# The last attention rounds beside the output projection, narrow products in halves, and an opening with its weight remainders on VectorE

## The chip, the cores and the metric

The kernel runs on one core of one Trainium2 chip. The metric is the device time of one execution in microseconds (us), as the median of three runs. One further execution was recorded by the hardware profiler; all rows below come from it.

## The reference

One inference step of a trunk of four layers, for a prompt of 256 positions and eight samples of one position each (264 columns together), width 1024. Each layer is a mixer and a SwiGLU feed-forward, each with a norm before and after and a residual sum. The mixers are retention (layers 0 and 3), pooling (layer 1) and dilated attention (layer 2):

```
for i in range(DEPTH):                       # 4
    kind, j = i % 3, i // 3
    hp, hs = rms_norm(xp, g[0]), rms_norm(xs, g[0])
    ...                                      # mixer(kind) of hp and of hs
    xp = xp + rms_norm(mp, g[1])
    xp = xp + rms_norm(swiglu(rms_norm(xp, g[2]), w_ffn_in[i], w_ffn_out[i]), g[3])
    ...                                      # the same for xs

# attention: 3 dilation groups (128, 1), (512, 4), (2048, 16), 16 heads of 64
proj = (xn @ w_in).reshape(B, L, G, 3, ATT_HEADS, ATT_DH)
    ...                                      # per group: scores + ALiBi bias, masked softmax, values
wts = jnp.stack(ls) * jnp.exp(m_all - jnp.max(m_all, axis=0))
o = jnp.einsum('gblh,gblhe->blhe', wts, jnp.stack(outs)) / jnp.sum(wts, axis=0)[..., None]
return o.reshape(B, L, D_MODEL) @ w_out, new_kv
```

For the prompt the keys are the prompt's own; for each of the eight samples they are rows of three caches and the sample's own row. Everything is float32.

## The kernel before

**Weights.** The activations stand with features on partitions and the 264 columns along the free axis. The weights come in units, mostly of 1024 x 256 (1 MB). SyncE loads unit u into one of three `raw` buffers as soon as the remainder of unit u - 3 is done (L404). To keep float32's accuracy, a unit is split in two: ScalarE rounds it to `w_hi` (`hi(u)`, L428), and VectorE or GpSimd computes the remainder `w_lo` = raw - w_hi (`lo(u)`, L917 and L1383). Which of them does it is set by the list `on_pool`: mostly odd units on GpSimd, in the retention layers nearly all. `w_hi` and `w_lo` have three buffers each; `hi(u)` waits until unit u - 3 has been used. The activations are split likewise (`g_hi`, `g_lo`).

**Projections.** A unit gives 256 output features, two halves t of 128, each in a bank of a pair of PSUM banks `acc`. `proj` issues, for each t and each of the eight input features blocks k, w_hi x g_hi and w_hi x g_lo (L1476, L1477), and then the w_lo x g_hi products (L1483): 48 products of 264 columns. Behind each t of the first pass, and behind t = 0 of the second, a function of a list `between` may issue other work. VectorE reads the banks.

**Queues.** Each engine has one stream, written out by hand; the engines meet in semaphores. There is no planner: the order in each stream is the order of the source. So an instruction waits behind everything before it on its engine.

**Opening.** TensorE first runs eight products of identity and ones (L1562) while the input lands, transposes the input (L1571, L1572), and then runs the high products of units 0 and 1 (`proj_first`, L1583, L1584). The column sums of the squares follow (`pre_stat`, L1538), then the low products of both units (L1590). VectorE copies the transposes (L1008, L1009), makes `g_lo` (L929), the remainder of unit 0, and two sums of squares (`pre_sum` L938, `pre_rest` L944) for which the column sums wait; unit 1's remainder is GpSimd's.

**Attention.** Sub-layer 4 has 36 input units, nine for each quad of four heads: query, key and value of three groups. They are steps n of 0 to 35. Each quad has eight rounds i (a head and a half of the prompt). A round is a chain over three engines: scores (PE, L1875), bias (DVE, L1248) and maximum (L1251), exp (ACT, L777), inverse of the sum (DVE, L1256), scaling (ACT, L783), three or six transposes (PE, L1859), their copy `pT` (ACT, L789), value products (PE, L1847), their copy `y` (DVE, L1239). `round_at(n)` says which round starts at step n; the eight rounds of a quad are spread over the steps of the next quad's units, with scores at n, transposes at n + 1, values at n + 2. From the second transpose on bank 1 they wait for the values of the round before to be copied.

The samples' attention of a quad, `decode(q, s)`, runs in steps s = 0 to 8 of the next quad, called on TensorE through `between`. Steps 1 to 4 spread two queries each over the partitions, and VectorE multiplies and sums them with the cached keys (L1269, L1272); steps 5 and 6 are the softmax; steps 7 and 8 are the value products, 16 each of 128x4 outputs with the cached values as stationary operand (L1914, two records each), in one block behind the first t of the projection.

For the last quad there is no next quad. Its first round starts at step 35; rounds 25 to 31 run in a loop of their own, `for i in range(24, 32)`, in which round i's transposes, round i - 1's values and round i + 1's scores stand beside one `decode(3, s)`. Scores alternate between the two pairs of `acc` banks. Behind the loop come the four units of the output projection: unit 0 in pieces (features 0 to 3, then the last round's values, then 4, 5, then 6, 7), as the attention's output features are split by `ao_hi` (ACT, L821) and `ao_lo` (DVE, L1305), and units 1, 2 and 3 whole (the last by `proj_last`). ScalarE does `hi(uo + p + 2)` ahead of unit p's square and gains (`post_square`), VectorE `lo(uo + p + 2)` ahead of reading unit p's banks (`post_evac`).

## Time and profile before

| | us |
|---|---|
| median of 3 runs | 1932.83 (1932.66 to 1934.03) |
| the profiled execution | 1937.19 |
| its span | 1935.4 |
| TensorE busy in the span | 1849.3 |
| VectorE, ScalarE, GpSimd busy | 1042.3, 911.4, 778.8 |
| mean granted TensorE clock | 0.966 |

The span is the time from the first to the last instruction; the profiled execution's own time has a little around it. Busy time of TensorE says nothing of its rate: the clock is granted at one of two levels, 1.2 or 2.4 GHz, and the windows below carry it as PEclk, with 1.00 for the full rate and 0.50 for the half. A record is one instruction as the profiler saw it; a float32 matmul shows as two records, a transpose as one.

### The profile page before, as it was taken

How to read it: one execution, taken by the hardware profiler on the slowest of the kernel's cores; microseconds unless marked ns; L12 is line 12 of the kernel's file. 1: busy time of each engine (PE TensorE's matmuls, PEld its weight loads, DVE VectorE, ACT ScalarE, POOL GpSimd, SP SyncE). 2: the span in 40 equal slices, each digit the busy share in tenths (PEclk: the TensorE clock that was granted, in tenths of full speed). 3: DMA queues.
4: the chain of work that ended last, by engine and by line, in shares of the span. 5: the costliest groups of instructions: out<-in, count | busy, mean ns of one | idle time of the engine just before them, and what ended most of it. 6: DMA issues, size and time to landing. Idle time of an engine off the chain costs nothing.

```text
span 1935.4 us, 32448 instructions
## 1 busy us (share of the span) xinstructions
PE 1849.3 (96%) x14116; PEld 1781.6 (92%) x14116; DVE 1042.3 (54%) x1119; ACT 911.4 (47%) x1064; POOL 778.8 (40%) x226
## 2 busy tenths in 40 slices
PE   8999989999979999999999979999999999899997
PEld 7999989999879999989989969999999999899997
DVE  5455554764487745354545452776354545647753
ACT  5556555343553344353434433544455555553333
POOL 5455435554224443412211200345455545355541
PEclk9999989999989999999999977999999999899999
DMA  8766855555335555844545521355667678545552
GB/s 266 251 227 245 290 176 172 175 174 180 104 109 177 182 184 167 244 149 134 162 135 154 143 69 43 127 184 164 189 229 238 231 252 294 184 143 175 174 180 83
DMA packets 306036, 346.33 MB, mean 179 GB/s; under 512 B 7847, under 2 KB 269479, under 8 KB 305887
## 3 DMA queue, kind: packets, MB, share of 16 engines
q1 hardware_dynamic: 257968, 260.36, 42.9%
q10 hardware_dynamic: 47927, 83.90, 12.6%
q8 instruction: 112, 1.84, 0.4%
q14 instruction: 29, 0.24, 0.0%
HBM read 299.66 MB, written 44.82 MB: 178 GB/s over the span
## 4 chain that ended last, share of the span: by engine, by line
PE 81%; DVE 9%; ACT 4%; issue 3%; DMA 2%; ACTq 1%; PEldq 0%; DVEq 0%
PE acc L1476 20%; PE acc L1477 20%; PE acc L1483 20%; PE mix L1914 2%; PE mix L1616 2%; PE mix L1875 1%; PE mix L1538 1%; DMA out_dram<-st 1%; PE acc L1504 1%; PE mix L1847 1%; ACT w_hi L428 1%; PE acc L1505 1%; PE acc L1510 1%; PE mix L1628 1%; DVE st L1029 1%
## 5 line engine op out<-in xcount | busy, mean ns | idle before, releaser
L1383 POOL TENSOR_TENSOR w_lo<-raw,w_hi 128x2048 fp32r<-128x2048 f32 (+2 forms) x163 | 695.1, 4268 | 728.6 <-ACT w_hi L428 728.6
L1476 PE MATMUL acc<-g_hi,w_hi 128*128 128x264 f32 x2576 | 658.0, 293 | 9.5 <-DVE gate L1172 3.2
L1477 PE MATMUL acc<-g_lo,w_hi 128*128 128x264 f32 x2576 | 646.8, 288 | 0.0
L428 ACT ACTIVATE w_hi<-raw 128x2048 fp32r<-128x2048 f32 (+3 forms) x260 | 455.9, 1755 | 166.7 <-PE acc L1483 78.3
L917 DVE TENSOR_TENSOR w_lo<-raw,w_hi 128x2048 fp32r<-128x2048 f32 (+1 forms) x97 | 376.2, 3878 | 270.4 <-ACT w_hi L428 270.4
L1476 PEld LDWEIGHTS acc<-g_hi,w_hi 128*128 128x128 f32 x2576 | 493.5, 192 | 18.5 <-issue 13.0
L1477 PEld LDWEIGHTS acc<-g_lo,w_hi 128*128 128x128 f32 x2576 | 496.4, 193 | 1.2
L1483 PE MATMUL acc<-g_hi,w_lo 128*128 128x264 f32 x2576 | 351.1, 287 | 0.0
L1483 PEld LDWEIGHTS acc<-g_hi,w_lo 128*128 128x128 f32 x2576 | 333.9, 190 | 1.5
L1416 POOL TENSOR_TENSOR h_lo<-hid,h_hi 128x528 fp32r<-128x528 f32 x44 | 59.2, 1344 | 333.5 <-ACT h_hi L702 333.5
L1476 PE MATMUL acc<-h_hi,w_hi 128*128 128x264 f32 x664 | 164.1, 284 | 0.0
L1477 PE MATMUL acc<-h_lo,w_hi 128*128 128x264 f32 x664 | 164.0, 285 | 0.0
L699 ACT ACTIVATE silu_gate<-gate 128x528 f32<-128x528 f32 x44 | 28.4, 646 | 281.9 <-DVE gate L1172 281.9
L1477 PEld LDWEIGHTS acc<-h_lo,w_hi 128*128 128x128 f32 x664 | 125.1, 188 | 0.0
L1476 PEld LDWEIGHTS acc<-h_hi,w_hi 128*128 128x128 f32 x664 | 125.0, 188 | 0.0
L1029 DVE SCALAR_TENSOR_TENSOR st<-mix,k_s,st 128x512 f32<-128x512 f32 x128 | 89.9, 744 | 6.2 <-ACT st L526 3.3
L1483 PE MATMUL acc<-h_hi,w_lo 128*128 128x264 f32 x664 | 90.7, 285 | 0.0
L1038 DVE SCALAR_TENSOR_TENSOR tq<-st,rq,mix 128x512 f32<-128x512 f32 x64 | 47.8, 747 | 71.3 <-ACT mix L537 45.1
L1483 PEld LDWEIGHTS acc<-h_hi,w_lo 128*128 128x128 f32 x664 | 84.9, 189 | 0.0
L526 ACT ACTIVATE st<-st 128x1024 f32<-128x1024 f32 x64 | 67.1, 1052 | 20.7 <-DMA st<-in_state_ret_dram 11.7
L1616 PEld LDWEIGHTS mix<-tbase,tq 128*128 128x128 f32 x512 | 65.4, 199 | 6.7 <-DVE tq L1038 4.0
L1616 PE MATMUL mix<-tbase,tq 128*128 128x1 f32 x512 | 64.4, 247 | 4.8 <-DVE tq L1038 4.7
(232 smaller groups left out, 2427.2 us busy)
## 6 DMA issues: line engine op xcount, KB each, us to landing
raw<-in_w_ffn_in_dram SPq DMA_DIRECT2D x88, 1024.0 KB, 5.3
raw<-in_w_in_ret_dram SPq DMA_DIRECT2D x48, 1024.0 KB, 6.8
raw<-in_w_in_attn_dram SPq DMA_DIRECT2D x36, 1024.0 KB, 5.5
st<-in_state_ret_dram ACTq DMA_DIRECT2D x64, 512.0 KB, 6.6
out_dram<-st ACTq DMA_DIRECT2D x64, 512.0 KB, 6.0
raw<-in_w_ffn_out_dram SPq DMA_DIRECT2D x32, 768.0 KB, 4.9
raw<-in_w_ffn_out_dram SPq DMA_DIRECT2D x32, 640.0 KB, 5.1
raw<-in_w_out_ret_dram SPq DMA_DIRECT2D x16, 1024.0 KB, 6.9
```

What stands on the lines that cost most here:

```text
L428: A(w_hi[:, u % SPL, 0:size[u]], raw[:, u % RAW, 0:size[u]], ACT.Copy).then_inc(hi_split, 1)
L526: A(st[:, g % ST], st[:, g % ST], ACT.Copy, scale=GAMMA[n // 8]).then_inc(st_scaled, 1)
L917: TT(w_lo[:, u % SPL, 0:size[u]], raw[:, u % RAW, 0:size[u]], w_hi[:, u % SPL, 0:size[u]].bitcast(F32), ALU.subtract).then_inc(lo_by_dve, 1)
L1029: ins = STT(st[:, g % ST, kt, :], mix[:, 2, :], k_s[:, n // 8 % 2, kt, b:b + 1], st[:, g % ST, kt, :], ALU.mult, ALU.add)
L1038: STT(tq[:], st[:, g % ST, 1, :], rq[:, n // 8 % 2, 1, SEQ + b:SEQ + b + 1], mix[:, 3, :], ALU.mult, ALU.add).then_inc(t_ready, 1)
L1383: TT(w_lo[:, u % SPL, 0:size[u]], raw[:, u % RAW, 0:size[u]], w_hi[:, u % SPL, 0:size[u]].bitcast(F32), ALU.subtract).then_inc(lo_by_pool, 1)
L1416: TT(h_lo[:, 2 * j:2 * j + 2, :], hid[:, j % 2], h_hi[:, 2 * j:2 * j + 2, :].bitcast(F32), ALU.subtract).then_inc(h_lo_ready, 1)
L1476: MM(out, wh, x_hi[:, ks[k], :], start=first and k == 0, stop=False)
L1477: MM(out, wh, x_lo[:, ks[k], :], start=False, stop=False)
L1483: ins = MM(acc[:, 2 * (pair % 2) + t, 0:T], w_lo[:, u % SPL, o:o + P], x_hi[:, ks[k], :], start=False, stop=last and k == len(ks) - 1)
L1616: ins = MM(mix[:, 0, vt * 8 + b:vt * 8 + b + 1], tq[:, vt * P:(vt + 1) * P], ones[:, 0:1], start=True, stop=True)
L1914: ins = MM(out, vc[:, b, x, t * P:(t + 1) * P], dPT[:, x, 4 * b:4 * b + 4], start=(x == 0), stop=(x == 1))
```

## The change

Four things change.

1. **Opening.** Unit 1's remainder is VectorE's (`on_pool`), issued behind the sum for the column sums. The products ahead of the input go from eight to four.
2. **Narrow products.** `decode` of steps 7 and 8 takes `parts`: four samples behind t = 0 of the unit's high products and four behind t = 1.
3. **Last quad.** The rounds of the last quad follow the spread of the others: steps 36 to 44 take the place of the loop, with scores at n, values of n - 2 and transposes of n - 1. Scores 25 to 31 go to the one pair of `acc` banks that output unit 1 uses later, and wait for the bias of the round before. Output unit 0 is started in the other pair: features 0 to 3 at steps 38 to 41, and features 4 and 5 at steps 43 and 44, between the halves of the narrow products. Behind the steps come unit 1's features 0 to 5, unit 0's 6 and 7, unit 1's 6 and 7, then units 2 and 3. VectorE puts the inverse between its two sample products, and copies the values behind the second. ScalarE issues `row_out(23)` behind the first scaling, and the new value rows' DMAs behind the next exp.
4. **`hi(uo + 2)`** moves from behind the last features' split to step 43.

```diff
-        on_pool += [n == 0 if next_pooled and n < 2 else
+        on_pool += [n == 0 if next_pooled and n < 2 else sub > 0 and u % 2 == 1 if n < 2 and not after else
...
-            return 8 * (m // 9) + m % 9 if m >= 0 and m % 9 < 8 else None
+            return 8 * (m // 9) + m % 9 if 0 <= m < 36 and m % 9 < 8 else None
+        def out_k_at(n):
+            return {38: 0, 39: 1, 40: 2, 41: 3, 43: 4, 44: 5}.get(n)
...
-            wide_bank = mix[:, 2:4, :] if i <= 24 else acc[:, 2 * (i % 2):2 * (i % 2) + 2, :]
+            late = (pair_at[ATT_SUB, "out"] + 1) % 2
+            wide_bank = mix[:, 2:4, :] if i <= 24 else acc[:, 2 * late:2 * late + 2, :]
...
# ScalarE
+                scaled(24)
                 row_out(23)
-                new_rows(3, 1)
-                decode(3, 0)
-                for i in range(24, 32):
...
+                for n in range(36, 45):
+                    if round_at(n) is not None:
+                        exps(round_at(n))
+                    decode(3, n - 36)
+                    if n == 36:
+                        new_rows(3, 1)
...
+                    if round_at(n) is not None:
+                        scaled(round_at(n))
+                    if 36 <= n < 42:
+                        ao_hi(n - 36)
+                    if round_at(n - 1) is not None:
+                        turned_out(round_at(n - 1))
+                    if n == 43:
+                        hi(uo + 2)
...
# VectorE
+                if sub == 0:
+                    lo(1)
                 lo(where[sub, "in"] + 2)
...
+                for n in range(36, 45):
+                    if round_at(n) is not None:
+                        biased(round_at(n))
+                    decode(3, n - 36, (0,))
+                    if round_at(n) is not None:
+                        inverse(round_at(n))
+                    decode(3, n - 36, (1,))
+                    if round_at(n - 2) is not None:
+                        pv_evac(round_at(n - 2))
+                    decode_end(3, n - 36)
+                    if 36 <= n < 42:
+                        ao_lo(n - 36)
...
# TensorE
-            for j in range(8):
+            for j in range(4):
                 MM(mix[:, 3, 0:P], ident, ones, start=True, stop=True)
...
-                        if i >= 27:
-                            pe.wait_ge(sc_biased, i - 1)
+                        pe.wait_ge(sc_biased, i)
...
-                        for b in range(DECB):
+                        for b in [4 * part + j for part in parts for j in range(4)]:
...
+                        split = (lambda: decode(quad - 1, s, (0,)), lambda: decode(quad - 1, s, (1,)))
                         proj(u0 + n, p0 + n, g_hi, g_lo, KK,
-                             between=(lambda: decode(quad - 1, s),) if quad else ())
+                             between=split if quad and s >= 7 else (lambda: decode(quad - 1, s),) if quad else ())
...
+                def out_part(p, ks, last=False):
+                    u, pair = uo + p, po + p
+                    pe.wait_ge(hi_split, u + 1)
+                    pe.wait_ge(lo_by_pool if on_pool[u] else lo_by_dve, lo_count[u])
+                    pe.wait_ge(acc_read, pair - 1)
+                    for k in ks:
+                        ao_wait(k)
+                        for t in range(2):
+                            out, at = acc[:, 2 * (pair % 2) + t, 0:T], k * UC + t * P
+                            wh = w_hi[:, u % SPL, at:at + P]
+                            MM(out, wh, g_hi[:, k, :], start=(k == 0), stop=False)
+                            MM(out, wh, g_lo[:, k, :], start=False, stop=False)
+                        for t in range(2):
+                            at = k * UC + t * P
+                            ins = MM(acc[:, 2 * (pair % 2) + t, 0:T], w_lo[:, u % SPL, at:at + P], g_hi[:, k, :],
+                                     start=False, stop=(k == KD - 1))
+                    if last:
+                        ins.then_inc(unit_done, 1)
...
+                for n in range(36, 45):
+                    if round_at(n) is not None:
+                        scores(round_at(n))
+                    if n > 36:
+                        decode_read(3, n - 37)
+                    decode(3, n - 36, (0,) if n >= 43 else (0, 1))
+                    if out_k_at(n) is not None:
+                        out_part(0, [out_k_at(n)])
+                    if n >= 43:
+                        decode(3, n - 36, (1,))
+                    if round_at(n - 2) is not None:
+                        values(round_at(n - 2))
+                    if round_at(n - 1) is not None:
+                        turn_probs(round_at(n - 1))
+                decode_read(3, 8)
                 pe.wait_ge(sc_biased, 32)
...
+                out_part(1, range(6))
+                out_part(0, (6, 7), last=True)
+                out_part(1, (6, 7), last=True)
+                proj(uo + 2, po + 2, g_hi, g_lo, KK)
                 proj_last(uo + 3, po + 3, g_hi, g_lo, KK, first=True)
```

## Rows read from the trace of the kernel before

**Rows 1.** The page, engines: busy us (share of the span) x instructions.

```profile
PE 1849.3 (96%) x14116; PEld 1781.6 (92%) x14116; DVE 1042.3 (54%) x1119; ACT 911.4 (47%) x1064; POOL 778.8 (40%) x226
```

**Rows 2.** TensorE's waits, whole span: waiting line, releaser: total us, times, longest.

```profile
PE mix L1859 <- DVE y L1239: 9.3, 9, 2.5
...
PE mix L1538 <- DVE sq L944: 2.7, 1, 2.7
```

**Rows 3.** Windows, opening: stretch, length, busy by engine (instructions), PEclk, DMA, GB/s.

```profile
13.00:21.00 8.00, 7.70 (x61) 7.45 (x62) 7.93 (x14) 7.99 (x12) 3.88 (x1) 1.00 0.49 147
...
24.40:32.10 7.70, 7.68 (x43) 7.28 (x44) 2.63 (x3) 2.46 (x3) 4.37 (x2) 0.78 0.93 300
```

**Rows 4.** Timeline, opening, several engines: start, us, instruction, [idle before <-releaser].

```profile
16.48 2.29 DVE L917 TENSOR_TENSOR w_lo<-raw,w_hi 128x2048 fp32r<-128x2048 f32 x1
...
17.12 6.68 POOL L1383 TENSOR_TENSOR w_lo<-raw,w_hi 128x2048 fp32r<-128x2048 f32 x1 [16.68 <-ACT w_hi L428]
...
18.68 0.71 DVE L938 TENSOR_TENSOR sq<-sq 128x528 f32<-128x528 f32 x1
...
19.09 1.90 ACT L428 ACTIVATE w_hi<-raw 128x2048 fp32r<-128x2048 f32 x1
...
19.43 4.94 DVE L944 TENSOR_TENSOR sq<-sq 128x528 f32<-128x528 f32 x1
...
24.42 1.76 PEld L1538 LDWEIGHTS mix<-sq,tbase 128*128 128x128 f32 x8 [2.95 <-DVE sq L944]
...
26.36 5.59 PE L1590 MATMUL acc<-g_hi,w_lo 128*128 128x264 f32 x32
```

**Rows 5.** Tile tbase, up to 15 us: ns min/median/max of warm-up, then transposes.

```profile
L1562 PE MATMUL mix<-tbase x16: 420/421/582, 4.9 to 8.3; 128*128 128x128 f32 x16
...
L1571 PE MATMUL mix<-tbase,y x16: 272/300/341, 8.7 to 12.7; 128*128 128x128 f32 x16
```

**Rows 6.** Windows around the narrow blocks of quads 1 to 3.

```profile
899.00:913.00 14.00, 13.87 (x93) 13.63 (x92) 5.35 (x9) 3.65 (x4) 0.00 (x0) 0.76 0.42 139
998.00:1010.00 12.00, 11.87 (x89) 11.63 (x88) 2.24 (x7) 4.13 (x5) 4.57 (x1) 0.86 0.22 74
1012.00:1022.00 10.00, 10.00 (x75) 9.96 (x75) 3.33 (x4) 0.99 (x3) 0.00 (x0) 0.83 0.57 149
1098.00:1108.00 10.00, 9.87 (x71) 9.63 (x71) 3.80 (x7) 2.92 (x4) 0.00 (x0) 0.83 0.31 109
1108.00:1120.00 12.00, 12.00 (x92) 11.96 (x91) 1.03 (x3) 2.93 (x3) 4.54 (x1) 0.86 0.43 118
```

**Rows 7.** Timeline of TensorE: a narrow block, a retention query; and a window around that.

```profile
1109.85 3.63 PE L1914 MATMUL mix<-sq,vc 128*128 128x4 f32 x32
...
132.04 1.02 PE L1616 MATMUL mix<-tbase,tq 128*128 128x1 f32 x8 [0.41 <-DVE tq L1038]
...
100.00:150.00 50.00, 48.86 (x370) 45.58 (x369) 23.69 (x31) 29.12 (x32) 24.10 (x7) 1.00 0.68 233
```

**Rows 8.** The last quad: three windows, and TensorE's longest waits from 1121 to 1184.

```profile
1121.00:1168.00 47.00, 36.15 (x160) 28.71 (x161) 29.29 (x58) 19.96 (x45) 0.00 (x0) 0.69 0.14 38
1168.00:1190.00 22.00, 22.00 (x105) 22.00 (x105) 1.38 (x6) 2.11 (x3) 0.00 (x0) 0.50 0.00 1
...
PE mix L1847 <- ACT pT L789: 4.2, 2, 3.3
PE mix L1859 <- DVE y L1239: 3.7, 3, 1.9
```

**Rows 9.** Timeline, output projection, three engines.

```profile
1198.03 2.13 PE L1483 MATMUL acc<-g_hi,w_lo 128*128 128x264 f32 x16
...
1198.73 1.90 ACT L428 ACTIVATE w_hi<-raw 128x2048 fp32r<-128x2048 f32 x1
...
1200.70 4.62 POOL L1383 TENSOR_TENSOR w_lo<-raw,w_hi 128x2048 fp32r<-128x2048 f32 x1 [85.39 <-ACT w_hi L428]
...
1203.88 2.13 PE L1483 MATMUL acc<-g_hi,w_lo 128*128 128x264 f32 x16
```

More of the change, by code:

```diff
@@ L854, in att_mixer @@
                         act.wait_ge(dpv_read, 6)
-                    if i < 30:
-                        ao_hi(i - 24)
-                    decode(3, i - 23)
+                    if round_at(n) is not None:
[6 more added lines that the diff above has]
+                        hi(uo + 2)
                 act.wait_ge(kv_stored, 16 * 12)
@@ L863, in att_mixer @@
                 for p in range(4):
-                    hi(uo + p + 2)
+                    if p:
+                        hi(uo + p + 2)
                     post_square(sub, p)
@@ L1256, in inverse, with decode @@
                     nc.vector.reciprocal(rl[:, i % 2:i % 2 + 1], lsum[:, i % 2:i % 2 + 1]).then_inc(rl_ready, 1)
-                def decode(q, s):
-                    if s == 0:
+                def decode(q, s, parts=(0, 1)):
+                    if s == 0 and 0 in parts:
                         dve.wait_ge(qs_hi, q + 1)
@@ L1262, in decode @@
                            ALU.subtract).then_inc(qs_ready, 1)
-                    if s == 1:
+                    if s == 1 and 0 in parts:
                         dve.wait_ge(kc_in, 16 * 3 * (q + 1))
@@ L1266, in decode @@
                     if 1 <= s <= 4:
-                        for b in (2 * s - 2, 2 * s - 1):
+                        for b in [2 * s - 2 + part for part in parts]:
                             dve.wait_ge(qb_done, 8 * q + b + 1)
@@ L1274, in decode @@
                                                          AX.X, ALU.add))
-                    if s == 4:
+                    if s == 4 and 1 in parts:
                         TT(dS, dS, dbias[:, :, 4 * q:4 * q + 4].unsqueeze(2).broadcast_to([P, 2, DECB, 4]),
                            ALU.add).then_inc(ds_ready, 1)
-                    if s == 5:
+                    if s == 5 and 0 in parts:
                         dve.wait_ge(ds_turned, q + 1)
@@ L1281, in decode @@
                             .then_inc(dmax_ready, 1)
-                    if s == 6:
+                    if s == 6 and 0 in parts:
                         dve.wait_ge(vc_in, 16 * 3 * (q + 1))
@@ L1335, in att_mixer @@
                 inverse(24)
-                decode(3, 0)
-                for i in range(24, 32):
-                    if i < 31:
-                        biased(i + 1)
-                    if i > 24:
-                        pv_evac(i - 1)
-                    if i < 31:
-                        inverse(i + 1)
-                    decode(3, i - 23)
-                    decode_end(3, i - 23)
-                    if 25 <= i <= 30:
-                        ao_lo(i - 25)
-                pv_evac(31)
+                for n in range(36, 45):
[10 more added lines that the diff above has]
+                        ao_lo(n - 36)
                 for k in (6, 7):
@@ L1878, in scores, with decode @@
                     scored[0] += 1
-                def decode(q, s):
-                    par = q % 2
+                def decode(q, s, parts=(0, 1)):
                     banks_free()
@@ L1915, in decode @@
                                          start=(x == 0), stop=(x == 1))
-                        ins.then_inc(dpv_done, 1)
+                        if 1 in parts:
+                            ins.then_inc(dpv_done, 1)
                 def ao_wait(k):
@@ L1937, in att_mixer @@
                         scores(round_at(n))
-                turn_rows(35)
-                decode(3, 0)
-                for i in range(24, 32):
-                    if i < 31:
-                        scores(i + 1)
-                    if i > 24:
-                        values(i - 1)
-                    turn_probs(i)
-                    decode_read(3, i - 24)
-                    decode(3, i - 23)
-                pe.wait_ge(sc_biased, 32)
-                proj(uo, po, g_hi, g_lo, [0, 1, 2, 3], last=False, ready=ao_wait, done=False)
@@ L1950, in att_mixer @@
-                values(31)
-                proj(uo, po, g_hi, g_lo, [4, 5], first=False, last=False, ready=ao_wait, at=4, done=False)
-                proj(uo, po, g_hi, g_lo, [6, 7], first=False, ready=ao_wait, at=6)
-                for p in (1, 2):
-                    proj(uo + p, po + p, g_hi, g_lo, KK)
+                def out_part(p, ks, last=False):
[16 more added lines that the diff above has]
+                        ins.then_inc(unit_done, 1)
```

7 lines of the change are left out of this document (removed).

## The prediction

> **What bounds the kernel now.** I read the page's engine table first: TensorE is busy for 96% of the span, so only what shortens TensorE's own stream, or the waits in it, can move the time [rows 1]. Then the waits of TensorE over the whole span: they are few and short, and two of them belong to places that the diff touches: the transposes of the probabilities wait 9.3 us in all for VectorE's copies out of the value products, and the statistics of the opening wait once for a sum on VectorE [rows 2]. Busy is not fast, however: the windows by stage carry the granted clock, and in three stages that the diff touches TensorE is fully busy at half of it. That, not idleness, is where most of the time lies.
>
> **Opening.** TensorE is idle for 2.95 us until 24.42 and comes back at a lower clock, 0.78 over the next 7.7 us [rows 3, 4]. The reader is to see why. VectorE's second sum (128x528) takes 4.94 us at 19.43 where the like one before it takes 0.71; it ends, at 24.37, 0.6 us after GpSimd's remainder of weight unit 1 (17.12 + 6.68 = 23.80). GpSimd's own 6.68 us holds the wait for VectorE's remainder of unit 0 (16.48 to 18.77). The two engines take turns on those instructions. In the SBUF page of the Trainium skill (SBUF — State Buffer, section "SBUF: two separate sides") this is an exclusive lock held for the whole instruction, against a VectorE instruction with two SBUF inputs; the trace agrees, 4.94 against 0.71 us.
>
> The change gives unit 1's remainder to VectorE, behind the sums. Step by step: unit 0's remainder ends at 18.77 as now; the two sums, 0.71 each, end at about 20.15; unit 1's remainder, 2.29, ends at 22.4. TensorE's first pass ends at 24.42 - 2.95 = 21.4 to 21.5, so its statistics start at once instead of at 24.42. Eight column sums and 32 low products now take until 26.36 + 5.59 = 31.95, that is 7.5 us with the lower clock. At full clock 16 low products take 2.13 us [rows 9], so 32 take some 4.1, and the column sums about 1.9: the end is at 21.4 + 6.0 = 27.4. **Gain 4.5 us.** GpSimd's next remainder (unit 2, ready at 19.09 + 1.90 = 20.99) must wait for VectorE until 22.4 instead of starting at 24.23; that costs nothing, as its products come last in TensorE's third unit. What is late next is the reciprocal behind the statistics, about 1 us behind TensorE at most.
>
> The same part halves the warm-up from 8 to 4 products (16 records to 8). They run before the input has landed and take no time themselves. They take 420 ns each by the record, the transposes after them 300 ns, 128 columns in both [rows 5]: the clock rose during them or at their end. With 4, TensorE stops at about 6.8 and waits until 8.7, and the transposes begin at half clock. The warm-up's 16 records start from 4.9 to 8.3, 0.23 us apart. The transposes take (12.7 - 8.7) / 7.5 = 0.54 us per feature, for three records and their pauses; with three records 0.23 apart and the pauses it is some 0.83, 0.29 us more each. If four or five of the eight are slow this is 1.3 us; none is 0, all eight 2.3. I take **a loss of 1.3**. The TensorE page of the skill (TensorE: Matmul & The Clock Gate, "Part 4: PE-mode transpose") says that transposes do not raise the clock, as they don't count as busy. Here the window that begins with the transposes' end keeps a clock of 1.00 after 4.3 us of nothing else [rows 3], so the trace speaks against it, at least for holding the clock. By the page the clock would stay low until the projection has run for a while, and the loss would be larger than my 1.3. Opening in all: **-3.2**, bounds -4.5 and +1 (the sum's gain and, against it, a slow first pass too).
>
> **Narrow products in halves.** In quads 1 to 3 six blocks of 32 records (128x4) stand inside a projection; one takes 3.4 to 3.6 us [rows 7]. Behind five of the six the clock halves. The windows around them give the loss as length x (1 - clock): 14 x 0.24 + 12 x 0.14 + 10 x 0.17 + 10 x 0.17 + 12 x 0.14 = **10.2 us** [rows 6]. TensorE is busy throughout, so a lost cycle is lost time. The change puts 16 records behind the first half of the unit's high products and 16 behind the second, 1.7 us each with 16 wide products (1.95 us) between. No record is added. The trace has no block of 1.7 us. Nearest from below: the retention's queries, 8 records of 128x1 in 1.02 us, many times, in a window with clock 1.00 [rows 7]. Nearest from above: 3.6 us, which costs 1.7. So the bounds are a gain of 10.2 and of 0 (and a loss, if each half brings a fall of its own; below). The halves are nearer to the 1.0 us, and each is framed by full-rate work of its own length; I take five of the six falls away: **-8.5**. VectorE sees the products' end 1.95 us later and then copies; TensorE waits for these copies only after the 16 low products, 2 us later, so nothing is added.
>
> **Last quad.** From 1121 to 1168 TensorE has 10.9 us without work and a clock of 0.69, from 1168 to 1190 it is fully busy at 0.50 [rows 8]. The waits are links of each round's chain (scores, bias, maximum, exp, inverse, scale, transposes, copy, values, copy): 4.2 us for the probabilities' copy, 3.7 for the values' copy [rows 8]. The change gives each link one more step and puts features 0 to 3 of output unit 0, 24 products, among steps 38 to 41. Now these stand behind the loop at half clock, about 5.8 us (at full rate 5.85 / 48 = 0.12 each, so 2.9). Features 4 and 5 go between the halves of the last two narrow blocks, where they run at half clock as TensorE has no gap there, and unit 1's first features take the place behind the loop. All products stay; a gain arises only as far as the moved ones fall into waits or lift the clock. Against it: scores go into one pair of banks instead of two, so each waits for the bias of the round before; the copy of the values stands behind both sample products on VectorE instead of ahead of them; the rows' DMA issues stand between an exp and its scaling on ScalarE. So I count on half of the 10.9 us remaining and the other half partly taken by these: **-3.3**, bounds -9.1 (5.8 and all of the 3.3 that the longest wait has) and +2.
>
> Then a new wait. Units 0 and 1 of the output now end 1.4 us apart (12 products), not a whole unit (1203.88 - 1198.03 = 5.85 us for 48). The high part of unit 3 stands on ScalarE behind unit 0's square and gains. With E the end of unit 1: unit 0 read out at E - 0.5; square and gains to E + 1.1; the high part 1.90 to E + 3.0; GpSimd's remainder 4.62 to E + 7.6 [rows 9]. Unit 2 ends at E + 5.85 and unit 3 needs the remainder: **+1.8**. Now it is there at 1205.32 for a start at 1203.88 + 2.13 = 1206.0, in time by 0.7. Last quad in all: **-1.5**, bounds -7 and +4.
>
> **Sum.** -3.2 - 8.5 - 1.5 = -13.2. The profiled execution took 1937.19 us (span 1935.4), 4.4 above the median of 1932.83; taken off the median, which is what is forecast: **1919.6, say 1920**.
>
> **Rivals.**
> *The clock falls all the same* behind the halves, once for each block: for it speaks that 4-column products are next to nothing to the array; against it that 1.02 us blocks never did it. The gain of 8.5 goes: 1928. Chance 0.12.
> *The last quad's rounds get slower*, because the single pair of banks and the later copies make chains longer than the features fill: VectorE has only 29.3 us of work in the 47, but in the steps with sample products nearly all of it. At the bound, +4 instead of -1.5: 1925.5. Chance 0.2.
> *The opening does not do what it says*: GpSimd gets in ahead of VectorE with unit 2's remainder (20.99 against 20.15, a margin of 0.85 us), or the slow transposes take all. Unit 1's remainder then ends at 21.0 + 4.6 + 2.3 = 27.9 and TensorE waits for it. The opening gives 0: 1923. Chance 0.1.
> *The other side*: every half-block brings its own fall. Its place is the six projections; the price 1.7 us per fall, so twelve falls, 20.4 us, against 8.5 now, and the two output features between the last halves change nothing. It decides once 1.7 us of narrow products suffice for a fall: then +10.2 instead of -8.5 and a total of +5.5: 1938. Chance 0.04.
>
> **Numbers.** The forecast holds 0.54. The range takes in the rivals at 1923, 1925.5 and 1928 and, below, all of the 10.2, the 4.5 without a loss and a last quad at -7 in part: 1910 to 1930. A measurement tells about 0.2% (3.9 us) from no change, so faster is below 1929. The forecast gives 0.54 faster, the opening rival 0.1, the slower rounds 0.17 of 0.2, the clock rival 0.07 of 0.12: faster 0.88. Same: 0.03 + 0.04, 0.07. Slower: the twelve falls 0.04 and 0.01 of the clock rival, 0.05.
>
> **What would show it.** Opening: VectorE's second sum at 0.7 us; TensorE without a wait before the statistics; the opening's 32 low products end near 28.5 instead of 31.95; transposes above 300 ns in part. Halves: clock 1.00 in the windows around the six blocks, each record group of 16. Last quad: the first output products before 1150, idle time in the rounds well below 10.9 us, the clock above 0.69; and a wait of some 1.8 us before the last output unit for GpSimd's remainder. Wrong, if the clock around the blocks stays near 0.8, or if the stretch from the last quad's first score to the end of output unit 1 is not shorter than now.

## The result and the profile after

The changed kernel takes **1916.3 us** (median of four runs, 1914.91 to 1918.46) against 1933.43 of the kernel before beside it (1932.66 to 1934.49): a ratio of 0.9912, 95% interval 0.9895 to 0.9929. That is 17.1 us less; forecast were 13.2 less. The profiled execution took 1915.92 us with a span of 1914.1, against 1937.19 and 1935.4, and its mean granted clock is 0.978, against 0.966.

The engine rows of the page after (those of before are [rows 1]):

```profile
PE 1828.6 (96%) x14108; PEld 1761.3 (92%) x14108; DVE 1039.6 (54%) x1120; ACT 910.9 (48%) x1064; POOL 773.9 (40%) x225
```

TensorE's busy time fell by 20.7 us with eight instructions fewer, as much as the span (21.3). So hardly a wait went away: the same instructions run faster. The windows place this. I give the part of a stage lost to half clock as length x (1 - PEclk), as in the prediction, here with PEclk before rounding. Over the span it is 65.6 us before and 41.6 after. Windows after, with the columns of [rows 3]: quads 0 to 3, then the last quad's rounds and its narrow blocks.

```profile
820.00:1108.00 288.00, 275.82 (x2164) 259.51 (x2164) 145.41 (x219) 126.05 (x183) 63.84 (x14) 1.00 0.52 150
1107.00:1154.00 47.00, 37.07 (x221) 30.93 (x220) 29.21 (x59) 21.40 (x46) 0.00 (x0) 0.83 0.24 60
1154.00:1176.00 22.00, 21.24 (x126) 20.95 (x126) 4.93 (x10) 3.46 (x5) 0.00 (x0) 0.67 0.14 49
```

The window of quads 0 to 3 in the kernel before:

```profile
820.00:1121.00 301.00, 289.28 (x2175) 272.68 (x2173) 145.86 (x218) 126.90 (x184) 65.16 (x15) 0.95 0.52 146
```

Between fixed marks, from record to record in the two timelines:

| stretch | before, us (lost to half clock) | after |
|---|---|---|
| start to the end of unit 1's low products | 31.9 | 30.7 |
| from there to the end of sub-layer 0 | 281.7 (5.1) | 282.9 (8.5) |
| first bias of quad 0 to that of quad 3 | 294.7 (13.7) | 282.9 (0.0) |
| last quad's first bias to the read-out of output unit 2 | 85.5 (25.6) | 77.7 (15.4) |

Between the end of sub-layer 0 and the first bias another 1.8 us went, in sub-layers that the diff does not touch: 8.5 us instead of 10.2 are lost to half clock there. All other stages agree within 0.3 us. What the opening gained, 1.2 us, was given back in sub-layer 0, where 3.4 us more are lost to half clock. Neither is the change's doing as far as is shown: over all profiles of this document, that part of sub-layer 0 loses between 3.4 and 10.2 us.

**The narrow blocks.** Windows around them, after (before: [rows 6]): the clock is 1.00 in each.

```profile
899.00:913.00 14.00, 13.87 (x118) 13.63 (x119) 3.90 (x7) 6.13 (x6) 2.14 (x1) 1.00 0.29 92
993.00:1005.00 12.00, 11.87 (x102) 11.63 (x101) 2.37 (x7) 5.55 (x6) 4.57 (x1) 1.00 0.28 89
1080.00:1105.00 25.00, 24.87 (x205) 23.97 (x204) 7.12 (x13) 7.61 (x9) 7.37 (x2) 1.00 0.30 97
```

**The opening.** Timeline of all engines, after:

```profile
4.85 2.08 PE L1571 MATMUL mix<-tbase 128*128 128x128 f32 x8 [4.85 <-DMA tbase<-in_t_base_dram]
9.04 0.69 PE L1580 MATMUL mix<-tbase,y 128*128 128x128 f32 x2 [2.11 <-DMA sq<-in_x_sample_dram]
...
24.86 1.94 PE L1547 MATMUL mix<-sq,tbase 128*128 128x264 f32 x8
...
26.45 4.25 PE L1599 MATMUL acc<-g_hi,w_lo 128*128 128x264 f32 x32
...
21.84 0.71 DVE L952 TENSOR_TENSOR sq<-sq 128x528 f32<-128x528 f32 x1
...
22.47 2.28 DVE L925 TENSOR_TENSOR w_lo<-raw,w_hi 128x2048 fp32r<-128x2048 f32 x1
...
22.82 6.36 POOL L1392 TENSOR_TENSOR w_lo<-raw,w_hi 128x2048 fp32r<-128x2048 f32 x1 [21.55 <-ACT w_hi L433]
```

VectorE's second sum takes 0.71 us instead of 4.94 [rows 4], and TensorE's statistics (L1547) have no wait in front. But they start at 24.86, not at 21.4: all that stands before is later. The tile's durations tell why (ns, min/median/max; [rows 5] before):

```profile
L1580 PE MATMUL mix<-tbase,y x16: 421/447/477, 9.0 to 15.2; 128*128 128x128 f32 x16
...
L1571 PE MATMUL mix<-tbase x8: 421/421/583, 4.9 to 6.5; 128*128 128x128 f32 x8
```

All sixteen transposes take some 447 ns, where 300 was the median before, and end at 15.6 instead of 13. The projection behind them starts at half clock too, until 18.4.

**The last quad.** The waits of TensorE from 1108 to 1175, after ([rows 8] before): in us the total, then how often, then the longest.

```profile
PE mix L1868 <- DVE y L1249: 4.6, 3, 2.1
PE mix L1900 <- DVE qs L1271: 1.5, 1, 1.5
PE mix L1907 <- DVE sq L1286: 1.3, 1, 1.3
PE mix L1893 <- ACT srow L765: 0.9, 1, 0.9
PE mix L1856 <- ACT pT L794: 0.8, 1, 0.8
PE acc L1957 <- DVE y L1310: 0.8, 1, 0.8
```

The probabilities' wait (4.2 us) is down to 0.8, but that for the values' copy is 4.6 and three small ones are new. With the two smallest, 0.7 and 0.2, they come to 10.8 us, against 10.9 us without work before. In this profile the time without work is no shorter than before; what the features fill is read from an experiment below. The timeline of the end of the output projection has the wait that was forecast: GpSimd's remainder of unit 3 ends at 1179.38 + 4.58 = 1183.96, and TensorE had been ready 1.62 us earlier.

```profile
1175.89 0.65 ACT L464 ACTIVATE sq<-y 128x528 f32<-128x528 f32 x1 [8.58 <-DVE y L973]
1177.40 1.90 ACT L433 ACTIVATE w_hi<-raw 128x2048 fp32r<-128x2048 f32 x1
...
1179.38 4.58 POOL L1392 TENSOR_TENSOR w_lo<-raw,w_hi 128x2048 fp32r<-128x2048 f32 x1 [76.07 <-ACT w_hi L433]
...
1184.06 0.36 PE L1535 MATMUL acc<-g_hi,w_hi 128*128 128x264 f32 x1 [1.62 <-issue]
```

So the last quad is 7.8 us shorter in this pair of profiles, with as much time without work. The experiments ask for the share of each part, for what keeps the clock, and for what the opening is short of.

### The profile page after: what moved, and what is told of

Its sections match the earlier page's. It is cut to its first block, busy times and chain, and to the rows that moved or that the text cites. A ratio compares the mean times of both kernels' runs of the same rounds, so it can differ in the third digit from the quotient of the medians.

```text
span 1914.1 us, 32457 instructions
## 1 busy us (share of the span) xinstructions
PE 1828.6 (96%) x14108; PEld 1761.3 (92%) x14108; DVE 1039.6 (54%) x1120; ACT 910.9 (48%) x1064; POOL 773.9 (40%) x225
## 3 DMA queue, kind: packets, MB, share of 16 engines
q8 instruction: 112, 1.84, 0.4%
## 4 chain that ended last, share of the span: by engine, by line
PE 82%; DVE 9%; ACT 4%; issue 2%; DMA 1%; ACTq 1%; PEldq 0%; DVEq 0%
PE acc L1485 20%; PE acc L1486 20%; PE acc L1492 20%; PE mix L1625 2%; PE mix L1921 2%; PE mix L1883 1%; PE mix L1547 1%; PE acc L1513 1%; ACT w_hi L433 1%; PE acc L1514 1%; DVE w_lo L925 1%; PE acc L1519 1%; PE mix L1856 1%; PE mix L1637 1%; PE mix L1714 1%
## 5 line engine op out<-in xcount | busy, mean ns | idle before, releaser
L1485 PE MATMUL acc<-g_hi,w_hi 128*128 128x264 f32 x2544 | 638.2, 289 | 8.7 <-DVE gate L1182 2.9
L1486 PE MATMUL acc<-g_lo,w_hi 128*128 128x264 f32 x2544 | 627.4, 284 | 0.0
L925 DVE TENSOR_TENSOR w_lo<-raw,w_hi 128x2048 fp32r<-128x2048 f32 (+2 forms) x98 | 381.1, 3888 | 269.0 <-ACT w_hi L433 269.0
L1485 PEld LDWEIGHTS acc<-g_hi,w_hi 128*128 128x128 f32 x2544 | 478.3, 188 | 17.2 <-issue 12.2
L1486 PEld LDWEIGHTS acc<-g_lo,w_hi 128*128 128x128 f32 x2544 | 480.8, 189 | 1.3
L1492 PE MATMUL acc<-g_hi,w_lo 128*128 128x264 f32 x2544 | 343.8, 285 | 0.6 <-POOL w_lo L1392 0.6
L1492 PEld LDWEIGHTS acc<-g_hi,w_lo 128*128 128x128 f32 x2544 | 325.9, 188 | 2.3 <-POOL w_lo L1392 0.8
```

What stands on the lines that cost most here:

```text
L925: TT(w_lo[:, u % SPL, 0:size[u]], raw[:, u % RAW, 0:size[u]], w_hi[:, u % SPL, 0:size[u]].bitcast(F32), ALU.subtract).then_inc(lo_by_dve, 1)
L1485: MM(out, wh, x_hi[:, ks[k], :], start=first and k == 0, stop=False)
L1486: MM(out, wh, x_lo[:, ks[k], :], start=False, stop=False)
L1492: ins = MM(acc[:, 2 * (pair % 2) + t, 0:T], w_lo[:, u % SPL, o:o + P], x_hi[:, ks[k], :], start=False, stop=last and k == len(ks) - 1)
```

## Experiments

All ratios are to the kernel before on the same chip, with 95% intervals. The first two sets ran on one chip, the third on another.

**First set: each part alone.** The kernel before ran at 1932.3 beside these.

*Only the halves* (the kernel before, plus):

```diff
...
-                        for b in range(DECB):
+                        for b in [4 * part + j for part in parts for j in range(4)]:
...
-                             between=(lambda: decode(quad - 1, s),) if quad else ())
+                             between=split if quad and s >= 7 else (lambda: decode(quad - 1, s),) if quad else ())
```

> The kernel before with one part of the change: the narrow sample products of quads 1 to 3 in two blocks of 16 records. Theory (the halves keep the clock): no half clock from 900 to 1118, the windows there at 1.00, and the time 10 to 12 us below the kernel before, about 1922. Rival (the clock moved for another reason, such as where the last quad begins): the windows keep falls behind the blocks and the time is within 3 us of before. Rival on the other side (each half a fall): about 1943.

Measured: 1922.7 us, 0.995 (0.993 to 0.997), 9.6 less by the medians, 5.8 to 13.5 by the interval. The stretch of quads 0 to 3 takes 284.4 us and loses 1.7 us to half clock, against 294.7 and 13.7. The one fall left (981 us) stands ahead of the block at 995, not behind a half. The halves do what was said, at the size that was said.

*Only the last quad* (the changed kernel, with the opening, `on_pool` with it, and the halves of quads 1 to 3 undone):

```diff
...
-                if sub == 0:
-                    lo(1)
...
-            for j in range(4):
+            for j in range(8):
...
-                             between=split if quad and s >= 7 else (lambda: decode(quad - 1, s),) if quad else ())
+                             between=(lambda: decode(quad - 1, s),) if quad else ())
```

> The kernel before with the last quad's steps, the output features among them and the two last narrow blocks in halves; opening and quads 1 to 3 as before. Theory: the stretch from the last quad's first bias to unit 2's read-out falls by some 7 us of which 1.8 are given back in the wait for the last output unit's remainder, about 1926. Rival (the gain of that stretch in the changed kernel came from a lucky clock, not from the order): within 3 us of before, 1931 or more.

Measured: 1929.7 us, 0.9985 (0.9968 to 1.0003): 2.6 less, not told from nothing by itself. In its profile the last quad's stretch takes 75.0 us, as in two more profiles of the changed order (77.7 in the first), while quads 0 to 3 lose 15.4 us to half clock.

*Only the opening* (the kernel before, with `on_pool` as changed, plus):

```diff
...
+                if sub == 0:
+                    lo(1)
                 lo(where[sub, "in"] + 2)
...
-            for j in range(8):
+            for j in range(4):
                 MM(mix[:, 3, 0:P], ident, ones, start=True, stop=True)
```

> The kernel before with the opening's part: unit 1's remainder on VectorE and four products ahead of the input. Theory (the sum on VectorE starts 4.5 us earlier, the slow transposes take 3 of them back): the opening's 32 low products end 1 to 1.5 us earlier and the time is 0 to 2 us below before. Rival (my prediction's term): 3.2 us below.

Measured: 1931.2 us, 1.0006 (0.9987 to 1.0026). The low products end at 30.9 instead of 31.9, and in the total nothing is to be seen (1.1 less by the medians, 1.2 more by the ratio).

*The changed kernel with eight warm-up products instead of four:*

```diff
-            for j in range(4):
+            for j in range(8):
```

> The changed kernel with eight products ahead of the input again, all else as changed. Theory (four products leave the clock at half through all transposes and the first of the projection, 3 us): transposes of 300 ns, the opening's low products end near 27.5, and the time 2 to 3 us below the changed kernel. Rival (what the opening gains is given back by the end of the first layer, where weights' transfers set the pace): the low products end near 27.5 but the time is the changed kernel's within 1 us.

Measured: 1912.3 us, 0.9905 (0.9879 to 0.9932). Its transposes are like those of before, and the low products end at 28.1, 2.6 us earlier than with four:

```profile
L1580 PE MATMUL mix<-tbase,y x16: 272/328/476, 9.3 to 13.4; 128*128 128x128 f32 x16
```

**Second set: what in the last quad's new order gains.** The kernel before: 1932.6.

*The changed kernel once more, without an edit:*

> The changed kernel once more, as the ground for the three others of this call. Theory and rival alike: 1916 within 3 us; the profile's clock falls may lie elsewhere than in its first profile, above all in the last quad and at the end of the first layer.

Measured: 1914.7 us, 0.9921 (0.99 to 0.9942).

*The old last quad* (the kernel before, with the halves of quads 1 to 3 and unit 1's remainder on VectorE, and eight warm-up products):

```diff
...
+                if sub == 0:
+                    lo(1)
...
-                             between=(lambda: decode(quad - 1, s),) if quad else ())
+                             between=split if quad and s >= 7 else (lambda: decode(quad - 1, s),) if quad else ())
```

> The kernel before with the narrow blocks in halves and the opening's remainder on VectorE with eight products ahead of the input; the last quad is the old loop. Theory (the last quad's new order is worth 1 to 3 us in the mean, the wait of 1.8 counted): 1 to 3 us above the changed kernel with eight products (1912.3), so about 1914 to 1916. Rival (the new order is the larger part of the gain, 7 to 8 us, as the two profiles show it between the first bias of the quad and the read-out of output unit 2): about 1920.

Measured: 1920.3 us, 0.9942 (0.9927 to 0.9958). That is where the rival of the expectation put it. The mean of its twelve runs is 1920.6. The changed kernel with eight warm-up products has a mean of 1916.0 over its twelve runs in two sets, and the changed kernel has 1915.2 in this set; so the new order is worth some 4.6 to 5.4 us in company, more than the 2.6 it showed alone. All of these have wide bounds.

This kernel also tests the opening again, with eight warm-up products, as it differs from the one with only the halves by nothing else. In its profile the low products end at 27.4 instead of 32.0, but the ratios are 0.9942 and 0.995: 1.5 us, again not told from nothing.

*The changed kernel without output features among the steps; they stand behind the loop:*

```diff
-            return {38: 0, 39: 1, 40: 2, 41: 3, 43: 4, 44: 5}.get(n)
+            return None
...
+                out_part(0, range(6))
                 out_part(1, range(6))
```

> The changed kernel with the first six features of output unit 0 behind the last quad's steps instead of among them; the steps' order and the read-out stay. Theory (the features fill TensorE's waits and shorten the stretch by what they take, 4.3 us at full clock, less what stands in no wait): 2 to 4 us above the changed kernel, and a lower clock in the steps. Rival (the steps are paced by VectorE's and ScalarE's chain, and TensorE's waits return elsewhere): within 1 us.

Measured: 1922.3 us, 0.9946 (0.9924 to 0.9968), with single executions from 1912.3 to 1926.9, where the changed kernel's six beside it lie between 1913.8 and 1917.1. By the medians the new order is worth nothing without the features: the time is that of the old last quad. One window of each kernel shows the difference (from the last quad's first bias to the read-out of output unit 2; the numbers after the length are busy times of PE, PEld, DVE, ACT and POOL, then PEclk). The kernel before:

```profile
1121.88:1207.39 85.51, 74.69 (x399) 67.27 (x400) 38.17 (x70) 31.39 (x58) 4.62 (x1) 0.70 0.12 34
```

The changed kernel:

```profile
1108.34:1186.03 77.69, 65.42 (x402) 59.12 (x403) 37.96 (x70) 31.38 (x58) 4.58 (x1) 0.80 0.18 46
```

The changed kernel without features among the steps:

```profile
1109.73:1193.29 83.56, 70.81 (x402) 63.80 (x403) 37.94 (x70) 31.38 (x58) 4.58 (x1) 0.75 0.17 43
```

The features do two things. In the rounds they fill waits. In the 42 us from 1109 on, this kernel and the changed kernel's second profile have the same clock, and TensorE is without work for 10.26 us without the features and for 7.94 with them, 2.3 us less:

```profile
1109.00:1151.00 42.00, 31.74 (x156) 25.23 (x156) 28.02 (x56) 19.06 (x42) 0.00 (x0) 0.76 0.25 62
...
1109.00:1151.00 42.00, 34.06 (x176) 27.81 (x177) 27.87 (x55) 19.18 (x42) 0.00 (x0) 0.76 0.26 64
```

Behind the rounds the clock differs. From the first of the last narrow blocks to the read-out of output unit 2, the kernel without features lost 10.2 us to half clock. The changed order lost 3.4 in three of its five profiles and 8.5 in two, the first among them.

Not all of the 7.8 us of the first pair of profiles is the order's, however. The kernel with only the opening has the last quad of the kernel before, instruction for instruction, and its profile shows this for the same stretch:

```profile
1116.76:1191.48 74.72, 64.29 (x399) 58.12 (x400) 38.02 (x70) 31.39 (x58) 4.62 (x1) 0.79 0.15 42
```

The four profiles of the old order have 85.5, 85.4, 79.4 and 74.7 us (25.6, 25.6, 23.9 and 15.4 lost), the five of the new order 77.7 twice and 75.0, 75.0 and 74.9 (15.4 twice, 13.7 three times). The means are 81.2 and 76.0, 5.2 us apart, which is near the timed difference.

Length times clock is what the stretch would take at full clock throughout, if no wait in it hid any of the loss: 59.9, 62.3 and 63.1 us for the three windows. Over the profiles it is 59.4 to 59.9 for three of the old order and 61.3 to 62.3 for the new one, so the changed order is some 2 us *longer* by this (the new wait of 1.6 us is most of it), and its gain is in the clock. The measure is rough: in the fourth profile of the old order it gives 55.5, because the half clock lay on the rounds and left TensorE only 6.0 us without work, where the others have 10.4 to 10.8.

*The new wait taken away* (the changed kernel, eight warm-up products, and unit 3's high part ahead of unit 0's square and gains on ScalarE):

```diff
+                hi(uo + 3)
                 for p in range(4):
-                    if p:
+                    if p > 1:
                         hi(uo + p + 2)
```

> The changed kernel with eight products ahead of the input, and the high part of output unit 3 issued ahead of output unit 0's square and gains on ScalarE instead of behind. Theory (the wait of 1.6 to 1.8 us before the last output unit is behind these 1.6 us of ScalarE): the wait goes, and the time is 4 to 5 us below the changed kernel, about 1911. Rival (another wait takes its place: output unit 1's gains come 1.9 us later and the end of the sub-layer waits for them): the time is that of the eight products alone, 1912.3.

Measured: 1916.0 us, 0.992 (0.9892 to 0.9947). The wait is gone: from the read-out of output unit 1 to that of unit 2 it takes 7.5 us instead of 9.4, and length times clock of the stretch is 58.5. The total shows nothing, and the profile shows two reasons. The stretch lost 18.8 us to half clock, against 13.7 to 15.4, and in the opening the clock fell again under the transposes. The window from 13 to 17 of this kernel:

```profile
13.00:17.00 4.00, 4.00 (x17) 3.56 (x18) 3.60 (x11) 4.00 (x8) 0.00 (x0) 0.50 0.69 219
```

The same window of the first kernel with eight warm-up products:

```profile
13.00:17.00 4.00, 3.70 (x27) 3.15 (x26) 3.96 (x14) 4.00 (x8) 0.00 (x0) 1.00 0.74 233
```

**Third set: which features count, and the best version.** The kernel before: 1934.1.

*Features 0 to 3 stay among steps 38 to 41, features 4 and 5 go behind the loop (nothing between the halves of the last two narrow blocks):*

```diff
-            return {38: 0, 39: 1, 40: 2, 41: 3, 43: 4, 44: 5}.get(n)
+            return {38: 0, 39: 1, 40: 2, 41: 3}.get(n)
...
+                out_part(0, (4, 5))
                 out_part(1, range(6))
```

> The changed kernel with features 0 to 3 of output unit 0 among steps 38 to 41 as changed, and 4 and 5 behind the steps instead of between the halves of the last two narrow blocks. Theory (the features between the narrow halves keep the clock up, and that is where the 6 us between the kernel without any features among the steps and the changed one lie): near the kernel without them, 1920 to 1922, with 6 to 10 us lost to half clock from the last narrow block on. Rival (the four features among the steps fill waits, and that is the gain): 1915 to 1917.

Measured: 1918.8 us, 0.9919 (0.99 to 0.9939), between the two values expected. The changed kernel with eight warm-up products took 1918.2 in this set (below), so features 4 and 5 between the halves show no worth of their own.

*The reverse: one feature between the halves of each of the last two blocks, none among the steps before:*

```diff
-            return {38: 0, 39: 1, 40: 2, 41: 3, 43: 4, 44: 5}.get(n)
+            return {43: 0, 44: 1}.get(n)
...
+                out_part(0, range(2, 6))
                 out_part(1, range(6))
```

> The changed kernel with features 0 and 1 between the halves of the last two narrow blocks and none among the earlier steps; 2 to 5 follow behind the steps. Theory (as for the run before): near the changed kernel, 1915 to 1918, with 3 to 5 us lost to half clock from the last narrow block on. Rival (the four among the steps are the gain): 1919 to 1922.

Measured: 1922.7 us, 0.9936 (0.9916 to 0.9957). The two totals' intervals overlap; the profiles speak more plainly. The stretch lost 15.4 us to half clock with the features among the steps (length 76.6), as much as the changed kernel, and 22.2 with those between the halves alone (84.8), near the kernel without any (20.5). Of these, 10.2 and 11.5 were lost ahead of the first of the last narrow blocks, and 5.1 and 10.6 from there on. So six wide products between two narrow halves don't keep the clock here. The 24 among the steps go with a clock that comes back sooner behind the rounds, not with a higher one in them; how they bring that about is not shown.

*Eighteen wide products between the halves* (the wait removed as above, eight warm-up products, and two features of output unit 1 beside each feature of unit 0):

```diff
...
                     if out_k_at(n) is not None:
                         out_part(0, [out_k_at(n)])
                     if n >= 43:
+                        pe.wait_ge(sc_biased, 32)
+                        out_part(1, (2 * (n - 43), 2 * (n - 43) + 1))
                         decode(3, n - 36, (1,))
...
-                out_part(1, range(6))
+                out_part(1, (4, 5))
```

> The changed kernel with eight products ahead of the input, the high part of output unit 3 ahead of unit 0's square, and two features of output unit 1 between the halves of each of the last two narrow blocks beside the one of unit 0 (18 products there instead of 6). Theory (more full-rate work between the halves keeps the clock more often): no half clock from the first of the last narrow blocks to the read-out of output unit 0, and the time 2 to 4 us below the changed kernel with eight products alone, about 1910. Rival (six products between the halves do it already, or the clock in the steps before has fallen and stays so through the blocks): the same as that kernel within 1.5 us.

Measured: **1909.2 us** (1906.4 to 1916.8), 0.9873 (0.9851 to 0.9895), the fastest of all here. Windows of this kernel, the rounds and then the narrow blocks:

```profile
1105.00:1147.00 42.00, 34.12 (x177) 27.90 (x177) 28.02 (x55) 19.24 (x42) 0.00 (x0) 0.76 0.26 60
1147.00:1167.00 20.00, 19.09 (x160) 18.33 (x159) 5.33 (x14) 6.07 (x9) 0.00 (x0) 1.00 0.01 1
1105.35:1175.56 70.21, 61.46 (x402) 54.67 (x403) 36.84 (x70) 31.57 (x58) 4.64 (x1) 0.85 0.21 53
```

Around the narrow blocks the clock stays at 1.00. The kernel nearest to it is the one with the new wait taken away, which has six products between the halves and the same features among the steps; the same 20 us of its profile:

```profile
1152.93:1172.93 20.00, 19.08 (x111) 18.58 (x110) 2.87 (x13) 5.68 (x8) 0.00 (x0) 0.64 0.00 1
```

The changed kernel has 0.63 there in its first profile (1150 to 1170) and 0.83 in its second (1151.5 to 1171.5). The whole stretch takes 70.2 us instead of 77.7, and loses 10.2 us to half clock, all of it in the rounds. With the features among the steps in all of them, none between the halves gives a loss of 15.4, six give 13.7 to 18.8 (six profiles), and eighteen 10.2.

*The changed kernel with eight warm-up products again:*

> The changed kernel with eight products ahead of the input, once more, as the ground for the run before and since single executions of one kernel spread by some 8 us. Theory: 1912 to 1914, 2 to 3 us below the changed kernel. Rival (eight products are worth nothing in the mean, since the clock's rise ahead of the first projection is a matter of luck): 1915 to 1916.

Measured: 1918.2 us, 0.992 (0.9891 to 0.9948), 5.9 above its first set, of which 1.8 are in the kernel before, too (1934.1 against 1932.3). In this profile the eight did not help: its transposes took 448 ns and the low products ended at 31.7.

```profile
L1580 PE MATMUL mix<-tbase,y x16: 421/448/475, 8.9 to 15.1; 128*128 128x128 f32 x16
```

## Why the prediction was right, and where it was not

**The bound.** The first reading held: TensorE's time at half clock, not its idleness, was what there was to win. The time lost to half clock fell by 24.0 us, the span by 21.3.

**Halves, forecast -8.5.** Right in mechanism and size: 9.6 us less alone, no half clock from 820 to 1108. The bound of 1.02 us for a harmless block and 3.6 for a harmful one enclosed the half (1.84 us), and to take it as nearer to the harmless end was right here. Every fall behind a block went, 10.2 us where I had taken 8.5: in the eleven profiles of kernels with halves in quads 1 to 3, no fall stands behind one. The table's 13.7 us hold 3.4 more, of two falls elsewhere (985 and 1074 us), which the change does not reach: zero, one or two of them are there in those eleven profiles, 0 to 3.4 us. The rivals in which the clock falls all the same, or twice as often, fell with it.

**Opening, forecast -3.2.** The first step was right: the sum is 0.71 us and the wait is gone. The step that failed is "a loss of 1.3" for the missing warm-up products. I had four or five of eight features slow at 0.29 us each. All eight were, and the projection behind them began at half clock as well: the statistics started at 24.86 instead of 21.4, 3.4 us late. That left 1.2 us of the 4.5, and alone it measured between -2.5 and +5.0. The forecast end of the low products, 28.5, was 30.7; the kernel with eight warm-up products reached 28.1. I had argued from a clock of 1.00 in the window after the transposes [rows 3] that transposes hold it and so might raise it. They held it there; they did not raise it. With four warm-up products the clock rose between 18.4 and 20.7 in all six profiles, only after the projection had begun. The rule in the Trainium skill that I had set aside (TensorE: Matmul & The Clock Gate, "Part 4: PE-mode transpose"), that transposes don't bring the full clock, would have given this, and the trace agrees with it here: sixteen transposes over 6.5 us at 447 ns. With eight the clock rose before 9.8 us in seven of eight profiles, and in two of those it fell again under the transposes. Timed, four and eight are not told apart: the changed kernel has a mean of 1915.7 over ten runs with four, and 1916.0 over twelve with eight.

**Last quad, forecast -1.5.** The sign was right, the size too small (-2.6 alone, interval -6.2 to +0.6; -4.6 to -5.4 in company), and the mechanism for the most part wrong. The step that failed is that half of the 10.9 us of waits goes. The features filled 2.3 us of them (7.94 against 10.26 without features, at the same clock), and the new wait of 1.6 us takes most of that back: over the whole stretch TensorE is without work for 12.3 us in two profiles of the new order and for 10.4 in three, against 10.4 to 10.8 in three of the old one. What was gained is clock. The stretch lost 13.7 to 15.4 us to it with the new order, and 15.4 to 25.6 with the old one. I had named "lift the clock" in half a sentence and given it no price. "They run at half clock" for features 4 and 5 did not hold: in the changed kernel's first profile their products start 0.12 us apart, the full rate (feature 4 from 1150.98, feature 5 from 1159.87), and in the reverse kernel those between one of its two pairs of halves do.

```profile
1160.07 0.28 PE L1958 MATMUL acc<-g_lo,w_hi 128*128 128x264 f32 x1
1160.19 0.28 PE L1957 MATMUL acc<-g_hi,w_hi 128*128 128x264 f32 x1
```

The new wait of 1.8 us was right, at 1.62, and it went in the two kernels that split unit 3 earlier. I had the rounds as possibly slower; by length times clock the stretch is some 2 us longer, which that wait mostly accounts for.

**The sum.** -13.2 against -17.1. The parts measured alone come to -13.3 by the medians (9.6 + 2.6 + 1.1) and to -11.4 by the ratios. The two errors, an opening of about -1 or nothing and a last quad of -3 to -5, offset each other: that the parts add up to the sum of the prediction is luck. What the whole has above its parts, 4 to 6 us, is not settled: each of these numbers has an interval of 3 to 4 us on either side.

**What stays open.** Single executions of one kernel lie up to 18 us apart in one set (the kernel before: 1920.4 to 1938.4), as the stretches at half clock fall differently. The same last quad took 74.7 us in one profile and 85.5 in another. Two kernels of the second and third set rest on one profile each for what they say of the clock behind the rounds (without features, and with features in the narrow blocks alone). Hence differences of 1 to 3 us between versions are not settled, among them how the fastest version's gain (9.0 us under the changed kernel with eight warm-up products in the same set) divides between the eighteen products, the wait and the opening.

## What to carry to other kernels

Where the page shows TensorE at 96% busy and a mean clock below 1, price the half-clock stretches first (length x (1 - PEclk) by window), and look for what stands in front of them: here blocks of 3.6 us of 4-column products, five of six of which cost 1.7 us or more each, and nothing in halves with 2 us of wide products between. When filler work is put among short products, count what it does to the clock beside what it does to the idle time. And a change that brings the ends of two units together should be followed down the other engines' queues: ScalarE's square ahead of a split cost 1.6 us on TensorE. Before a stage's gain in one pair of profiles is believed, look at that stage in every other profile that has the same code: here the old last quad alone ranged over 10.8 us.

## What the runs showed of the hardware beyond that

With six products of 264 columns between two halves of 16 narrow ones the clock over the 20 us around the last narrow blocks was 0.63 to 0.83 in six profiles, with eighteen 1.00 in one, where TensorE had waited for 8 to 10 us in the rounds ahead. In the projections of quads 1 to 3, busy on both sides, it was 1.00 with sixteen. What a narrow block costs was read from its surroundings here, not from its own length alone. Ahead of the trace's first record of a clock (8.8 us before, 18.4 after) the windows print 1.00 whatever it was; there only the durations, 421 to 447 ns against 272 for 128 columns, tell the level.
